# A hybrid encoder step: index products set inside a projection tile, and output tiles begun inside the last attention rounds

## What is computed

```python
for i in range(4):
    kind = i % 3                        # 0 sparse attention, 1 RWKV-7, 2 latent attention
    x = x + mixer(kind, rmsnorm(x))
    x = x + conv_ffn(rmsnorm(x))        # gated MLP, width 2816, causal depthwise conv

def sparse(h):                          # layers 0 and 3
    q, k, v, qi, ki, wi = split(h @ w_in)
    score = sum_h wi[h] * relu(qi[h] @ ki_all.T)      # 8 index heads
    sel = top_k(score, 64)              # per segment, causal over chunks
    o = softmax(q @ k_all[sel]) @ v_all[sel]          # 16 heads, 2 key heads
    return o @ w_out

def latent(h):                          # layer 2, 16 heads, one joint latent
    ...
    return softmax(q @ k.T) @ v @ w_out
```

## Time and profile before

| | |
|---|---|
| three runs | 1753.55, 1754.89, 1755.53 us; median 1754.89 |
| the profiled execution | 1747.19 us in all, span from first to last instruction 1745.4 us |
| mean granted TensorE clock | 0.983 of 2.4 GHz |
| TensorE, VectorE, ScalarE, GpSimd busy | 95%, 66%, 49%, 43% of the span |
| sparse layer 0, scores to end of output projection | about 56 to 165 us |
| latent layer, attention rounds and output projection | about 1045 to 1124 us |
| sparse layer 3, the same as layer 0 | about 1390 to 1499 us |

### The profile page before, as it was taken

How to read it: one execution, slowest core, us unless ns; L and a number is a source line. 1 busy time by engine, 2 the same in 40 slices (tenths; PEclk the granted TensorE clock), 3 DMA queues, 4 the chain that set the end, 5 groups by cost and what they waited for, 6 DMA issues and landing times.

```text
span 1745.4 us, 37515 instructions
## 1 busy us (share of the span) xinstructions
PE 1657.7 (95%) x14117; PEld 1571.1 (90%) x14117; DVE 1155.0 (66%) x2061; ACT 856.4 (49%) x1604; POOL 742.6 (43%) x815
## 2 busy tenths in 40 slices
PE   6989999996988997999999998999999999999998
PEld 5869999994878997999999887999999977999998
DVE  5686777637477455677764738677765486777753
ACT  4474665433653433366643446465543445556633
POOL 5662666310045210366621446266631754466600
PEclk9999999998999998999999999999999999999999
DMA  7314555453330002455445311355545521555443
GB/s 204 105 51 118 161 144 144 133 156 99 97 106 23 10 4 81 128 155 151 137 133 167 123 45 65 111 155 144 146 133 156 155 82 49 145 151 154 130 136 113
DMA packets 344994, 205.11 MB, mean 118 GB/s; under 512 B 22456, under 2 KB 342312, under 8 KB 344752
## 3 DMA queue, kind: packets, MB, share of 16 engines
q1 hardware_dynamic: 342640, 199.76, 39.8%
q0 software_dynamic: 2080, 3.67, 0.8%
q10 hardware_dynamic: 160, 0.10, 0.0%
HBM read 200.02 MB, written 3.39 MB: 117 GB/s over the span
## 4 chain that ended last, share of the span: by engine, by line
PE 83%; DVE 10%; ACT 3%; issue 2%; POOL 1%; DMA 0%; SPq 0%; DVEq 0%; ACTq 0%; POOLq 0%
PE bank L910 24%; PE bank L911 23%; PE bank L912 23%; PE bank L1293 5%; PE bank L922 1%; DVE lo L2081 1%; DVE SW L2274 1%; ACT hi L1584 1%; DVE LS L2124 1%; DVE top L2271 1%; PE bank L1317 1%; DVE SC L2260 1%; DVE LS L2133 1%; PE bank L1232 1%; PE bank L944 0%
## 5 line engine op out<-in xcount | busy, mean ns | idle before, releaser
L910 PE MATMUL bank<-XH,hi 128*128 128x320 f32 (+1 forms) x1976 | 624.6, 316 | 9.4 <-DVE lo L2081 3.2
L2081 DVE TENSOR_TENSOR lo<-raw,hi 128x2048 fp32r<-128x2048 f32 (+4 forms) x197 | 419.9, 2132 | 299.5 <-ACT hi L1584 299.5
L911 PE MATMUL bank<-XL,hi 128*128 128x320 f32 (+1 forms) x1976 | 614.9, 311 | 0.0
L912 PE MATMUL bank<-XH,lo 128*128 128x320 f32 (+1 forms) x1976 | 614.7, 311 | 0.0
L1584 ACT ACTIVATE hi<-raw 128x2048 fp32r<-128x2048 f32 (+4 forms) x205 | 359.8, 1755 | 74.5 <-PE bank L912 63.5
L910 PEld LDWEIGHTS bank<-XH,hi 128*128 128x128 f32 (+1 forms) x1976 | 373.2, 189 | 24.1 <-issue 9.0
L911 PEld LDWEIGHTS bank<-XL,hi 128*128 128x128 f32 (+1 forms) x1976 | 373.6, 189 | 1.5 <-issue 0.2
L912 PEld LDWEIGHTS bank<-XH,lo 128*128 128x128 f32 (+1 forms) x1976 | 373.1, 189 | 0.0
L715 POOL TENSOR_TENSOR upad<-upad,rstd 128x128 f32<-128x128 f32 (+1 forms) x176 | 168.0, 974 | 199.5 <-ACT upad L1663 199.5
L910 PE MATMUL bank<-GH,hi 128*128 128x322 f32 x704 | 219.8, 312 | 0.0
L911 PE MATMUL bank<-GL,hi 128*128 128x322 f32 x704 | 218.7, 311 | 0.0
(11 more groups left out here) (384 smaller groups left out, 2378.7 us busy)
## 6 DMA issues: line engine op xcount, KB each, us to landing
raw<-in_f_w_up SPq DMA_DIRECT2D x176, 512.0 KB, 5.0
raw<-in_f_w_down SPq DMA_DIRECT2D x64, 704.0 KB, 4.7
raw<-in_a_w_in SPq DMA_DIRECT2D x12, 1024.0 KB, 5.3
raw<-in_b_w_rkv SPq DMA_DIRECT2D x12, 1024.0 KB, 5.1
raw<-in_a_w_out SPq DMA_DIRECT2D x8, 1024.0 KB, 5.1
raw<-in_b_w_out SPq DMA_DIRECT2D x4, 1024.0 KB, 5.6
raw<-in_c_w_out SPq DMA_DIRECT2D x4, 1024.0 KB, 5.1
raw<-in_a_w_in SPq DMA_DIRECT2D x12, 256.0 KB, 4.7
```

What stands on the lines that cost most here:

```text
L910: pe.matmul(out, a, xh(k), start=(start and k == 0), stop=False)
L911: pe.matmul(out, a, xl(k), start=False, stop=False)
L912: last = pe.matmul(out, b, xh(k), start=False, stop=(stop and k == kt - 1))
L2081: dve.tensor_tensor(lo[n % 2][:, 0:w_], raw[n % 2][:, 0:w_], hi[n % 2][:, 0:w_].bitcast(F32), ALU.subtract).then_inc(w_lo, 1)
```

## The change

Sparse layers: (1) tile 9 is cut in two halves of four k-tiles, and `dots(2)` stands between them; (2) of tile 15 only the products with hi stand before `pair_qk(1)`, those with lo behind it; (3) two output tiles are begun instead of three, tile 0 in round 6 over six k-tiles and tile 1 in round 7 over seven, and none in round 5; (4) POOL's eight pieces of lo are made one in round 4, two in round 5, two in round 6 and three in round 7, where it was one in rounds 3 and 4 and two in each of rounds 5 to 7; (5) ACT rounds output slab 2 before the square of tile 1, no more behind it.

Latent layer: (6) output tiles 0 and 1 are begun in rounds 6 and 7, and the layer uses `attention_out` with its three banks; (7) the second output slab is rounded by ACT at the end of round 4 and subtracted by DVE at the end of round 5; slab 2 is split on both engines around tile 1, as in the sparse layers.

```diff
@@ POOL, sparse layer, round p
-                        if p in (3, 4):
-                            split_lo(out, p - 3, p - 2)
+                        if p == 4:
+                            split_lo(out, 0, 1)
                         if p == 5:
-                            split_lo(out, 2, 4)
-                        if p >= 6:
-                            split_lo(out + 1, 2 * p - 12, 2 * p - 10)
+                            split_lo(out, 1, 3)
+                        if p == 6:
+                            split_lo(out, 3, 4)
+                            split_lo(out + 1, 0, 1)
+                        if p == 7:
+                            split_lo(out + 1, 1, 4)
@@ PE
             def out_begun(layer, m):
-                n, end = first_slab[layer, "out"] + m // 2, 5 + m
+                n, end = first_slab[layer, "out"], 6 + m
@@ PE, attention_out
-                            ... first=(5, 6, 7, 0)[min(m, 3)])
+                            ... first=(6, 7, 0)[min(m, 2)])
@@ PE, sparse layer
                 dots(0)
                 dots(1)
-                project(9)
+                ready(s0 + slab_of[9])
+                pe.wait_ge(tile_evac, E + 8)
+                tile_part(9, 0, 4)
                 dots(2)
+                tile_part(9, 4, None)
                 dots(3)
...
                 for t in range(10, 15):
                     project(t)
                 pair_qk(0)
-                tile_15()
+                tile_15(False)
                 pair_qk(1)
-                tile_16(0, 4)
+                tile_15(True)
+                pe.wait_ge(tile_evac, E + 15)
+                tile_part(16, 0, 4)
                 pair_qk(2)
                 for p in range(PAIRS):
                     turn_probs(Q + p)
                     if p + 3 < PAIRS:
                         pair_qk(p + 3)
-                    else:
-                        out_begun(layer, p - 5)
+                    elif p > 5:
+                        out_begun(layer, p - 6)
@@ PE, latent layer, round p
+                    if p > 5:
+                        out_begun(layer, p - 6)
                     values(Q + p, vals)
...
-                mixer_out(layer, lambda k: OH[:, k, :], lambda k: OL[:, k, :], lambda: pe.wait_ge(ol_done, Q + PAIRS))
+                attention_out(layer)
@@ ACT, mixer_out(layer, split)
                 for m in range(KD):
-                    if m % 2 == 0 and m // 2 >= split:
+                    if split and m == 1:
+                        split_hi(s0 + 2)
+                    if m % 2 == 0 and m // 2 >= 2 * split:
                         split_hi(s0 + m // 2 + 1)
@@ ACT, latent layer, end of round p
+                    if p == 4:
+                        split_hi(s0 + 10)
-                mixer_out(layer)
+                mixer_out(layer, 1)
@@ DVE, latent layer, end of round p
-                    if p in (1, 3):
+                    if p in (1, 3, 5):
                         split_lo(s0 + 8 + p // 2)
-                mixer_out(layer)
+                mixer_out(layer, 1)
```

More of the change, by code:

```diff
@@ L1003, in attention_out @@
                     product(psum[out_bank(m)][:, 0:T], n, 128 * (m % 2), lambda k: OH[:, k, :], lambda k: OL[:, k, :],
-                            before=(lambda k: pe.wait_ge(ol_done, q + k + 1)) if m == 0 else None, first=(5, 6, 7, 0)[min(m, 3)])
+                            before=(lambda k: pe.wait_ge(ol_done, q + k + 1)) if m == 0 else None, first=(6, 7, 0)[min(m, 2)])
             def mixer_out(layer, xh, xl, wait):
@@ L1157, in dots, with tile_part @@
                     sample(1).then_inc(dots_done, 1)
+                def tile_part(t, first, end):
+                    product(psum[q_bank(t)][:, 0:T], s0 + slab_of[t], col_of[t], lambda k: XH[:, k, :], lambda k: XL[:, k, :],
+                            first=first, end=end)
                 dots(0)
                 dots(1)
-                project(9)
+                ready(s0 + slab_of[9])
+                pe.wait_ge(tile_evac, E + 8)
+                tile_part(9, 0, 4)
                 dots(2)
+                tile_part(9, 4, None)
                 dots(3)
@@ L1168, in pair_qk, with tile_15 @@
                     qk(Q + p, lambda e: QD[64 * e:64 * e + 64, p, :], lambda e: KT[64 * e:64 * e + 64, p // 4, :], 64)
-                def tile_15():
+                def tile_15(low):
                     n = s0 + slab_of[15]
@@ L1173, in tile_15 @@
                     out, c = psum[q_bank(15)][:, 0:T], slice(col_of[15], col_of[15] + 128)
[L1174 to L1188, removed]
+                    if low:
+                        ready(n)
+                        for k in range(KD):
+                            last = pe.matmul(out, wl[:, k, c], XH[:, k, :], start=False, stop=(k == KD - 1))
+                        last.then_inc(mm_done, 1)
+                    else:
+                        pe.wait_ge(w_hi, n + 1)
+                        pe.wait_ge(tile_evac, E + 14)
+                        for k in range(KD):
+                            pe.matmul(out, wh[:, k, c], XH[:, k, :], start=(k == 0), stop=False)
+                            pe.matmul(out, wh[:, k, c], XL[:, k, :], start=False, stop=False)
                 for t in range(10, 15):
@@ L1200, in dsa @@
                         pair_qk(p + 3)
-                    else:
-                        out_begun(layer, p - 5)
+                    elif p > 5:
+                        out_begun(layer, p - 6)
                     if p < 2:
-                        tile_16(4 + 2 * p, 6 if p == 0 else None)
+                        tile_part(16, 4 + 2 * p, 6 if p == 0 else None)
                     g = slice(64 * (p // 4), 64 * (p // 4) + 64)
```

## The result

The changed kernel takes 1741.0 us (median of 20 executions, 1733.4 to 1747.9), the kernel before 1751.2 (20 executions, 1746.3 to 1757.9). The medians differ by 10.1 us; the ratio is 0.9935, 95% interval 0.9923 to 0.9947: 0.65% faster, where I had forecast 0.26% and a range that ended at 0.38%. The sign was right, the size was not. The forecast started from a median of three executions of before, 1754.89, all in the upper half of its spread: over 20 the median is 3.7 us lower. The profiled executions are 1747.19 us (span 1745.4) and 1737.47 us (span 1735.6): 9.8 us apart.

A forecast was written before the change was run, and what follows sets the result against it. TensorE, busy 95% of the span, was taken to bound the kernel. Two sparse layers at -1.5 us each and the latent layer at -1.5 gave -4.5 us: 1750.4 from a median of 1754.89, range 1748.3 to 1753.8.

The forecast's parts named there:

- Selection (part 1): Index products, each sparse layer: earlier dots(2) lets the selection on DVE gain 0.8 us, bounds nothing and 1.8.
- the bracket ahead of `pair_qk(1)`: Sparse layer, TensorE's wait for the maxima: expected to grow from 1.05 to about 1.7 us.
- Tile 15 (part 2): Each sparse layer: low products between the pairs make pair_qk(2) start 0.4 us later.
- GpSimd's piece (part 4): Round 3 of each sparse layer: without POOL's piece beside DVE's division, 0.8 us saved; bounds 0 and 0.9.
- Last rounds and slab 2 (parts 3, 5): End of each sparse layer: 3.4 us of waits removed, 2.3 added, sum -1.1; bounds -0.5 and -2.0.
- Latent layer (parts 6, 7): Latent layer's end: 2.7 us of brackets removed, new waits added, sum -1.5; bounds -0.8 and -2.0.
- All rivals: Short clock falls 0.27, long or many falls 0.10, sparse layers giving nothing 0.10, more from the selection 0.08.
- The clock takes it back: Rival: new gaps in sparse layers bring one or two short clock falls, 1752.1 or 1753.8 us; chance 0.27.
- the 1034 fall: Kernel before, after a 2.04 us gap and logits: clock at 1.2 GHz for four windows, lost shares 1.7 us.
- the fall at the index products: Kernel before, from 61.00 after small transposes and a short gap: clock fall over seven windows, 3.4 us.
- The step that the fall would follow a stop in the rounds: Sparse layers: new gaps of 1.7 to 1.8 us are followed by a clock fall of 1.7 us; rival's chance 0.27.

The follow-up runs named there:

- e1: The kernel before with only tile 9 cut in halves around dots(2); ratio to before 1.0011.
- e6: The kernel before with parts 1 and 2 alone: tile 9 in halves, tile 15's low products behind pair_qk(1); ratio to before 1.0003.
- t5: The changed kernel with high products first and more covers at OL and in the latent layer, but tiles 9 and 15 whole; ratio to before 0.9892.
- e2: The changed kernel with part 1 undone, tile 9 whole again ahead of dots(2); ratio to before 0.9970.
- u4: The changed kernel with part 4 undone, GpSimd's pieces in the rounds of before; ratio to before 0.9958.
- c1: The changed kernel with idle ScalarE rounding ahead of slab 2, putting back a stop of 1.38 us there; ratio to before 0.9964.
- c0: The changed kernel itself, run again as the measure for later runs; ratio to before 0.9939.
- t2: The changed kernel with the first half of tile 9 moved ahead of dots(0); ratio to before 0.9936.
- c2: The changed kernel with idle ScalarE rounding ahead of slab 2, making a stop of 1.94 us there; ratio to before 0.9974.
- c3: The changed kernel with idle ScalarE rounding ahead of slab 2, making a stop of 2.48 us there; ratio to before 0.9988.
- e5: The kernel before with parts 3, 4 and 5 alone, tiles 9 and 15 whole, latent layer as before; ratio to before 0.9961.

## Why the prediction was wrong in size

**Selection (part 1).** Forecast 0.8 us, measured 1.06, near for the wrong reason. Its shape I had read from a fall: of the 3.87 us of idle time before head 4 about 3 belonged to products at 1.2 GHz ahead of `dots(2)`. So in the changed kernel nothing is left before head 4, and 0.47 before head 6 where I had said 2 and 1. The score itself ends 0.50 us earlier. The other 0.57 is the operation behind it, which no longer runs beside GpSimd's (0.29 us for 0.86); the sum had no term for it. One more change from dense products to small matmuls and back costs TensorE 7.48 - 6.83 = 0.65 us (e1), not 0.2. With both the bracket ahead of `pair_qk(1)` comes out: 2.50 - 1.06 - 0.65 = 0.79, where I had 1.7.

**Tile 15 (part 2).** Forecast +0.4 at `pair_qk(2)`, measured +0.12 at equal clock (38.24 for 38.12); between the two pairs stand 1.18 us more, as forecast. Together the two parts are worth nothing: e6 and t5 show it, and e1 shows it of part 1. e2 shows that part 2 without part 1 costs.

**GpSimd's piece (part 4).** Forecast -0.8, measured -0.79, and u4 gives it back to 0.08 us. Right in mechanism and size. Of the two waits only the transposes' vanished; the query's went from 0.79 to 0.56. The Trainium skill's rule (SBUF — State Buffer, "Who interferes with whom") agrees: the division takes 1.24 us again with no GpSimd work beside it.

**Last rounds and slab 2 (parts 3, 5).** This is the term of the sum that failed most: "-1.1; bounds -0.5 and -2.0". Every bracket came as forecast. But the stretch from `turn_probs(5)` on fell from 39.23 to 37.44 us, 1.79. I priced waits at their brackets and left out those that show none. The starts in the two traces give the missing 0.7: the stop at slab 2 cost 2.11, not 1.84, which is c1's 0.26; tile 6, the first of slab 3, began 0.33 us after the product before it and its second product 0.26 later, 0.29 lost in all; and tile 2, begun in round 7, came 0.20 later behind the transposes than the begun tiles of the changed kernel. There tile 2 follows tile 1, and tile 6 tile 5, without any of this. In the kernel before, with 157.60 in the earlier trace rows:

```profile
157.27 0.31 PE L912 MATMUL bank<-OH,lo 128*128 128x320 f32 x1
```

**Latent layer (parts 6, 7).** Forecast -1.5, measured -1.82. The brackets are 0.36, none and 0.42.

At equal clock the stretches give 2 x (101.51 - 99.05) + 1.8 = 6.7 us (before at a full clock: 34.84 + 3.28 + 24.16 + 4.77 + 10.30 + 24.16 = 101.51); all executions give 6.5. Forecast: 4.5. Every term came inside its own bounds, but these add up to -9.0 us (per sparse layer -0.6 - 0.9 - 2.0, latent -2.0), and the range stopped at -6.6. With this alone the time would be 1754.89 - 6.7 = 1748.2, at the end of the range.

**The starting point.** 1754.89 was the median of three executions, all in the upper half of the spread; 20 give 1751.2. That is 3.7 us of the 13.9 between 1754.89 and the measured 1741.0. The forecast took the same saving off a median of three without asking how it is spread.

**The clock.** 3.8 us of the gain; the sum of the prediction has no term for it. All rivals let the clock take time, none let it give some: "The clock takes it back" named the 1034 fall and the fall at the index products, and took them as fixed parts of the kernel before. They were not. The index products' fall shows in 14 of 34 sparse layers over 17 traces: in both layers of before, in neither of the changed kernel, in one of c0, which is the same program. In layer 0 it begins before the last of the first dots, ahead of tile 9, and all kernels but t2 run the same instructions up to there; so there it comes and goes by execution, not by the order. The step that the fall would follow a stop in the rounds, which gave it 0.27, did not occur in the changed kernel's trace.

Why the mean clock is higher (0.9835 for 0.9807, over 26 and 93 executions) stays open. The stop at slab 2 was my candidate: e1, c2 and c3 show a fall behind it in six of six layers, but before and e6 in none of four, and c2, which has both stop and fall, keeps the changed kernel's mean clock. The runs only narrow it down: the three kernels that end their sparse layers as before did (before, e1, e6) have 0.980 to 0.981, the thirteen with parts 3 and 5 have 0.982 to 0.987. Without the other changes (e5, which has part 4 too) they reach 0.982, half of the way, with a standard error of 0.001, so they are not shown to carry all of it.

## What to carry to other kernels

A stop of TensorE costs more than its bracket, 0.26 us here, and a late operand can cost 0.2 to 0.3 us without any bracket, so measure a stretch from one matmul to the same one in the other trace, and do not add up brackets. Before reading an idle time as an order's fault, look at the clock in the stretch before it: a fall makes everything behind it look late. Where a change is below 1%, take the starting time from many executions, not three, and compare at equal clock. A wait for the second half of an operand (here lo) can be covered by the products that need only the first.

## What the runs showed of the hardware

The granted clock varies from execution to execution of one kernel, 0.979 to 0.989 in 20 of the changed one, and with it the span, 1746.1 to 1731.6 us. Over the 252 executions it goes with 86% of the variance within a kernel. A microsecond missing by the clock costs 0.76; the fall at the index products of before, 3.4 us missing, cost 3.06, that at 1034, 1.7 missing, 1.2. That the rest falls on waits is my reading; no run tests it.

Which stop is followed by a fall depends on more than its length. At slab 2, between dense products: 1.38 us, none of two; 1.84 to 1.86, two of six; 1.94 and 2.48, four of four. Ahead of `pair_qk(1)`: 1.81 us (t2, layer 0) and 2.50 (e2, both layers), three of three. In round 5, between small matmuls, a stop of 1.83 has a fall in one of 20 layers. The Trainium skill (TensorE: Matmul & The Clock Gate, "A second HAM failure mode: psum-queue depth-cycling") reports swings where many short stops stand between groups of matmuls. The rounds are of that kind, and a fall begins in them in one of 34 sparse layers.

Operations of VectorE take longer beside GpSimd's: the masking operation 0.86 us for 0.29, the division 2.10 for 1.24.
